# Layer 0 of a two-block transformer: gate tiles and modulation products set among the attention steps, and a reordered start

## The chip, the cores and the metric

The kernel runs on one core of a Trainium2 chip. It is written engine by engine: TensorE (PE) multiplies, VectorE (DVE) and ScalarE (ACT) work element by element, GpSimd (POOL) does elementwise work and issues some transfers, and SyncE (SP) issues the rest. Each engine runs its own list in order, and semaphores are what holds them together. The metric is the device time of one launch in microseconds. Lower is better.

## The reference

Two transformer blocks of two layers each work on 256 tokens of width 1024, all in float32. Only layer 0 of the first block is touched, with the prologue that leads to it:

```python
mod = silu_c @ w_mod[l] + b_mod[l]; mod_c = silu_cc @ w_mod[l] + b_mod[l]     # 1024 -> 6144, for the tokens and for the context
h  = modulate(rms_norm(x, norm1[l]), sh1, sc1);  hc = modulate(rms_norm(ctx, norm1[l]), csh1, csc1)
na_q, na_k, na_v, gq, gk, gv, ga, gb = split(h @ w_in[l])                     # and the same of hc
ya = window attention of 8 heads, 64 wide, with bias, over 256 tokens and 256 context tokens
ob = grouped attention of 8 query heads and 2 key heads, q and k normed per head and rotated
x  = x + g1 * ((sigmoid(ga) * (ya @ w_pa) + sigmoid(gb) * (ob @ w_pb)) @ w_o) # layer 0 does the same for the context
```

`ga` and `gb` are the gates, 1024 features each. The modulation is a product of one row per stream with a 1024 x 6144 matrix: it costs 24 MB of weights a layer and nearly no arithmetic.

## The kernel before, in words

**The plan.** `Plan` holds a list of items written out by hand. Every engine walks that list and does its own part of each item, in order. So the order of the `add` calls, and of the generators that make them, is the order on every engine. There is no scheduler behind it.

**Weights.** A weight piece is 128 x 2048 floats (1 MB) or less, loaded by SP into a ring of four slots (`piece`, L162). The load of piece n is issued when piece n - 3 has begun on TensorE (L1045 to L1053). A piece that is multiplied with h is split: ACT copies it, rounded, to `w_hi`, and DVE writes the rest over the slot as `ring_lo`; three products (hi by hi, lo by hi, hi by lo) replace one product in float32. `ahead` (ACT L1511, DVE L1983) does the splits up to the count that `look_ahead` (L175) wrote into the piece: one split piece ahead, if it lies at most three pieces further on. A modulation piece isn't split.

**Feature tiles.** `feat` (L488) makes tiles of 128 output features by 512 columns (256 tokens and 256 context tokens): 24 products of 128 x 512 in `product` (L1114), then a copy by ACT (L1644). Two tiles come from a 1 MB piece. The 16 gate tiles are eight pieces of `w_in`. Tiles are written into three PSUM banks in turn (`linear`, L158). The copies of gates 0 to 7, 8 to 11 and 12 to 15 go over the window attention's queries and keys, its values, and its bias.

**Modulation.** Unit j of `mod_unit` (L341) makes 2048 of the 6144 outputs from eight steps `mod` (L1228); a step is a 1 MB piece and four products of 32 columns wide weights side by side. DVE copies the sum, TensorE turns it onto the partitions (`mod_turn`, L1256), and DVE adds the bias. Unit 0 is made in the start. Unit 1 takes its pieces not from the ring but from `logits` and `prob_t`, which POOL fills by turns (`mod_loads`, L1898), each load when the buffer's last piece has been used.

**The start** (`first_tiles`, L587). ACT squares eight chunks, DVE adds six of them (L2010), TensorE sums over the partitions (L1166), and from the roots come the normed rows. `rows` are the modulated chunks of h (ACT L1568, DVE L2059 and L2051), two chunks at a time for the low part. `parts(i, c)` (L1213) adds chunk c to the two tiles of piece i. `mod_in` (L1182) and `turn` (L1194) make the modulation of each half of the chunks. The second half stands after tile piece 0's first four parts.

**Layer 0** (`first_block`, L655): two steps of unit 1, four key tiles with the other six among them, the tile of the grouped values, unit 1's turn, the window values (`tok`, L1300), and then attention. An attention step `att` is two heads by 128 queries; step i makes its scores (L1352), then the values of step i - 3 (L1378), then the turned probabilities of step i - 2 (L1363). DVE takes the scores from PSUM with the minimum (L2345, with bias L2347), ACT exponentiates (L1726), DVE inverts (L2357), POOL scales (L1918). Steps 0 to 7 and 16 to 23 have 512 keys, the others of the 32 have 256. Steps 0 to 4 run among the last five feature tiles (gk, gq), steps 5 to 18 beside the head norm (`head_sums` L1313, `head_spread` L1325), the rotation (`rope` L1333) and the eight steps of modulation unit 2, one at a time. From step 20 on each call is followed by one gate tile. `merge1` comes behind.

Of the kernel before, what the change touches and what calls it, by code (L numbers as in the profile page):

```python
# [13 lines left out]
P = 128  # L14
# [127 lines left out]
class Plan:  # L142

    def __init__(self):
        self.items, self.pieces, self.splits = [], [], []
        self.full, self.taken, self.lin, self.counts = [0] * 8, [0] * 8, 0, {}
        self.in_slot = [0] * RING
# [10 lines left out]
    def linear(self):  # L158
        self.lin += 1
        return self.fill((self.lin - 1) % LIN)  # L160
# [14 lines left out]
    def look_ahead(self):  # L175
        done = 0
        for p in self.pieces:
# [4 lines left out]
            if nxt and nxt.s < own + 1 and nxt.n <= p.n + RING - 1:  # L182
                done += 1
# [3 lines left out]
def hybrid_kernel(nc, xt, vec_d, con_d, tables_d, rpb, w, out):  # L187

    with ExitStack() as ctx:
# [151 lines left out]
        def mod_unit(l, j, aside=False, f=None, f2=None):  # L341
# [12 lines left out]
            add("mod_turn", l=l, j=j, of=f, f=f2 or fill(TURN_BANK))  # L354
# [232 lines left out]
        def first_tiles(f):  # L587
# [46 lines left out]
            parts(0, 0, 1, 2, 3)  # L634
            mod_in(1, (0, 0), (0, 1))
            parts(1, 0, 1)
            mod_in(1, (1, 0), (1, 1))
            parts(1, 2)
            turn(1)
            parts(1, 3)  # L640
# [14 lines left out]
        def first_block(l):  # L655
# [44 lines left out]
            for u in range(8):  # L700
# [8 lines left out]
            if l == 0:  # L709
                unit, loads = mod_unit(0, 1, True), mod_loads(0, (1,), (logits, prob_t), turned)  # L710
                some(loads, 2)
                first_tiles_out(first)
                in_turn(unit, loads, 2)
                for t in nk:
                    for i, _ in enumerate(t):
                        in_turn(unit, loads, 1 + i)
# [4 lines left out]
                some(unit, 1)  # L721
# [7 lines left out]
                unit = mod_unit(0, 2, f=linear(), f2=linear())  # L729
                head_squares(hn, 0, 1, 2, 3)  # L730
                att(g)
                some(unit, 1)
                head_squares(hn, 4)
                att(g)
                some(unit, 1)
                head_sums(hn)
                att(g)
                some(unit, 1)
                att(g)
                some(unit, 1)  # L740
                head_spread(hn, 0, 1, 2)
                att(g)
                some(unit, 1)
                head_spread(hn, 3, 4)
                att(g)
                some(unit, 1)
# [3 lines left out]
                some(unit, 1)  # L750
                rope(ropes[3:], 1, need=(hn["last"],))
                att(g)
                some(unit, 1)
                add("ahead", p=plan.pieces[-1])
                last_mod = unit
# [3 lines left out]
                some(last_mod, 1)  # L759
                while g["i"] < 19:  # L760
                    att(g)
            else:
# [299 lines left out]
        def _(pe):  # L1062
# [96 lines left out]
            def pe_first_norm(st):  # L1159
                n = st["n"]  # L1160
                room(n["f"])
                pe.wait_ge(first_added, KC - 2)
                pe.wait_ge(squares, KC)
                for t in range(4):
                    for c in (0, KC - 1):
                        mm = pe.matmul(ps[n["f"].bank][:, t:t + 1], y1[:, c * SQ + t * P:c * SQ + (t + 1) * P], ones[:, 0:1],  # L1166
                                       start=c == 0, stop=c == KC - 1)
# [5 lines left out]
            def pe_first_mod(st):  # L1173
# [5 lines left out]
                unread((22, 2, 0, 0, 0, 0, 0, 0)[i])  # L1179
# [1457 lines left out]
```

## Time and profile before

| | us |
|---|---|
| median of 3 runs (2540.3 to 2549.95) | 2547.2 |
| the profiled execution | 2547.93 |
| its span in the profile | 2546.1 |
| PE busy | 2465.5 (97%) |
| DVE busy | 1427.2 (56%) |
| ACT busy | 1132.8 (44%) |
| POOL busy | 360.0 (14%) |
| mean granted clock of TensorE | 0.988 |

The span is the profile's own; 1.8 us lie around it. A busy PE isn't a full one: matmuls overlap, their ends are modelled, and a matmul at the lower clock counts as busy for twice as long. So the stretches in which PE is less than full, or its granted clock less than 1, are what is to be looked for.

### The profile page before, as it was taken

What the parts mean: (1) busy time and instruction counts of PE and PEld (TensorE: products, weight loads), DVE (VectorE), ACT (ScalarE), POOL (GpSimd) and SP (SyncE); (2) the same over time, 40 slices, a digit from 0 to 9 for tenths busy, and PEclk for the clock granted to TensorE, in tenths of its full rate; (3) what the DMA queues carried; (4) which work ended last, traced back from release to release, by engine and by line L of the source; (5) the groups of instructions that cost most, each with busy time, mean ns of one, the idle gap of its engine ahead of it and who ended that gap; (6) DMA issues with size and microseconds to landing.
All of it is one profiled execution on the core that took longest, in us unless ns stands there. A gap on an engine that the chain in (4) does not pass through costs nothing.

```text
span 2546.1 us, 41134 instructions
## 1 busy us (share of the span) xinstructions
PE 2465.5 (97%) x17098; PEld 2207.8 (87%) x17098; DVE 1427.2 (56%) x2394; ACT 1132.8 (44%) x1960; POOL 360.0 (14%) x354
## 2 busy tenths in 40 slices
PE   8988999999999999999999998999999999999998
PEld 6753778888888877899999998999999998899998
DVE  5234335574446445555566567576556556657654
ACT  3243443421222535554454444465445444447443
POOL 0233313100001305200100000240000000024000
PEclk9997999999999999999999999999999999999999
DMA  7622123353444332345565453355455454335543
GB/s 289 225 87 87 61 83 133 115 172 134 150 170 167 133 100 83 133 166 177 171 210 185 165 166 119 128 180 182 167 191 189 167 190 139 115 125 196 183 163 136
DMA packets 82697, 390.32 MB, mean 153 GB/s; under 512 B 14992, under 2 KB 23472, under 8 KB 52176
## 3 DMA queue, kind: packets, MB, share of 16 engines
q1 hardware_dynamic: 73136, 347.78, 40.2%
q0 software_dynamic: 9376, 39.91, 4.5%
q8 instruction: 136, 2.23, 0.4%
q14 instruction: 49, 0.40, 0.1%
HBM read 386.62 MB, written 1.05 MB: 152 GB/s over the span
## 4 chain that ended last, share of the span: by engine, by line
PE 87%; DVE 6%; ACT 5%; issue 2%; DMA 1%; POOL 0%; SPq 0%; DVEq 0%; POOLq 0%; ACTq 0%
PE ps L1114 74%; PE ps L1300 2%; PE ps L1378 2%; DVE ring_lo L1991 2%; PE ps L1363 2%; PE ps L1352 2%; ACT logits L1726 1%; ACT w_hi L1521 1%; PE ps L1213 1%; ACT prob_t L1733 0%; DMA arena<-w_mod 0%; PE ps L1325 0%; PE ps L1228 0%; PE ps L1313 0%; PE ps L1147 0%
## 5 line engine op out<-in xcount | busy, mean ns | idle before, releaser
L1991 DVE TENSOR_TENSOR ring_lo<-ring,w_hi 128x1024 fp32r<-128x1024 f32 (+3 forms) x704 | 763.8, 1126 | 328.5 <-ACT w_hi L1521 328.4
L1114 PE MATMUL ps<-h_hi,w_hi 128*128 128x256 f32 (+1 forms) x3392 | 936.0, 307 | 3.4 <-issue 1.6
L1114 PE MATMUL ps<-h_lo,w_hi 128*128 128x256 f32 (+1 forms) x3392 | 923.3, 304 | 1.5 <-DVE h_lo L2166 1.5
L1521 ACT ACTIVATE w_hi<-ring 128x1024 fp32r<-128x1024 f32 (+3 forms) x704 | 633.2, 947 | 411.3 <-PE ps L1114 374.4
L1114 PEld LDWEIGHTS ps<-h_hi,w_hi 128*128 128x128 f32 x3392 | 648.0, 192 | 44.6 <-issue 18.3
L1114 PEld LDWEIGHTS ps<-h_lo,w_hi 128*128 128x128 f32 x3392 | 648.4, 192 | 26.0 <-DVE h_lo L2166 1.7
L1114 PE MATMUL ps<-h_hi,ring_lo 128*128 128x256 f32 (+1 forms) x3392 | 558.1, 303 | 2.5 <-DVE ring_lo L1991 2.5
L1114 PEld LDWEIGHTS ps<-h_hi,ring_lo 128*128 128x128 f32 x3392 | 480.7, 192 | 27.4 <-DVE ring_lo L1991 3.0
L1114 PE MATMUL ps<-hid_hi,w_hi 128*128 128x256 f32 (+1 forms) x1078 | 290.1, 299 | 0.0
L1114 PE MATMUL ps<-hid_lo,w_hi 128*128 128x256 f32 (+1 forms) x1078 | 289.5, 298 | 0.0
L1918 POOL TENSOR_SCALAR logits<-logits,stat 128x512 f32<-128x512 f32 (+2 forms) x140 | 161.3, 1165 | 593.7 <-DVE stat L2357 593.7
L1114 PEld LDWEIGHTS ps<-hid_hi,w_hi 128*128 128x128 f32 x1078 | 206.3, 191 | 7.6 <-issue 1.7
L1114 PEld LDWEIGHTS ps<-hid_lo,w_hi 128*128 128x128 f32 x1078 | 206.3, 191 | 6.0
L2250 DVE TENSOR_TENSOR prob_t<-prob_t,ps 128x256 f32<-128x256 f32 (+1 forms) x132 | 61.5, 466 | 266.3 <-issue 236.4
L1873 POOL TENSOR_TENSOR logits<-logits 128x256 f32<-128x256 f32 (+1 forms) x71 | 61.9, 872 | 1045.1 <-ACT logits L1542 822.0
L1114 PE MATMUL ps<-hid_hi,ring_lo 128*128 128x256 f32 (+1 forms) x1078 | 181.5, 298 | 0.0
L1726 ACT ACTIVATE logits<-logits,stat 128x512 f32<-128x512 f32 (+2 forms) x140 | 81.5, 583 | 186.1 <-DVE logits L2345 88.7
L1114 PEld LDWEIGHTS ps<-hid_hi,ring_lo 128*128 128x128 f32 x1078 | 153.1, 191 | 6.0
L1679 ACT ACTIVATE prob_t<-prob_t 128x256 f32<-128x256 f32 x88 | 36.7, 417 | 161.4 <-DVE prob_t L2243 161.4
L1352 PE MATMUL ps<-arena 64*128 64x512 f32 (+2 forms) x280 | 69.0, 529 | 9.2 <-DVE logits L2345 6.6
L1114 PE MATMUL ps<-y_lo,w_hi 128*128 128x256 f32 (+1 forms) x272 | 77.7, 308 | 0.0
L2280 DVE SCALAR_TENSOR_TENSOR x_res<-ps,mod,x_res 128x256 f32<-128x256 f32 x64 | 29.1, 480 | 84.2 <-PE ps L1114 84.2
(287 smaller groups left out, 2416.0 us busy)
## 6 DMA issues: line engine op xcount, KB each, us to landing
ring<-w_ffn_in SPq DMA_DIRECT2D x132, 1024.0 KB, 4.9
ring<-w_ffn_out SPq DMA_DIRECT2D x96, 704.0 KB, 4.0
ring<-w_in SPq DMA_DIRECT2D x36, 1024.0 KB, 4.8
ring<-w_w_in SPq DMA_DIRECT2D x28, 1024.0 KB, 4.9
bias_t<-w_mod POOLq DMA_DIRECT2D x24, 1024.0 KB, 5.4
ring<-w_up SPq DMA_DIRECT2D x16, 576.0 KB, 3.7
ring<-w_mod SPq DMA_DIRECT2D x8, 1024.0 KB, 5.6
ring<-w_pab SPq DMA_DIRECT2D x8, 1024.0 KB, 4.9
```

What stands on the lines that cost most here:

```text
L1114: mm = pe.matmul(ps[fs[k].bank][:, at_col:at_col + n], (hi_w if wpart == "hi" else lo_w)[0:rows, at[k]:at[k] + P], hi if part == "hi" else ...
L1300: mm = pe.matmul(ps[f.bank][:, 0:st["n"]], at_T(part, c, T, t * P, P), wt[:, at:at + st["n"]], start=c == 0 and part is h_hi and wt is w_h ...
L1352: pe.matmul(ps[f.bank][:, 0:sp_["nk"]], p["q"][a, t * P:(t + 1) * P], p["k"][a, k0:k0 + sp_["nk"]], start=True, stop=True).then_inc(psum_f ...
L1363: mm = pe.transpose(ps[f.bank][:, c * P:(c + 1) * P], logits[:, o:o + P], ident)
L1378: mm = pe.matmul(ps[f.bank][DH * h:DH * h + DH, o:e], p["v"](c, h), prob_t[:, h * 1024 + c * S + o:h * 1024 + c * S + e], start=start, sto ...
L1521: act.activation(w_hi[q.s % 2][:, h * n:(h + 1) * n], ring[q.slot][:, h * n:(h + 1) * n], ACT.Copy)\
L1679: act.activation(t, t, ACT.Silu).then_inc(silu_done, 1)
L1726: act.activation(lg, lg, ACT.Exp, scale=-1.0, bias=stat[:, o:o + 1], accum_out=stat[:, 4 + o:5 + o])\
L1873: pool.tensor_tensor(sq_sum[:, o:n], sq_sum[:, o:n], sq[j % 2][:, o:n], ALU.add).then_inc(sq_added, 1)
L1918: pool.tensor_scalar(lg, lg, stat[:, 8 + (a % 2) * 2 + h:9 + (a % 2) * 2 + h], None, ALU.mult)\
L1991: dve.tensor_tensor(ring_lo[q.slot][:, c], ring[q.slot][:, c], plain(w_hi[q.s % 2][:, c]), ALU.subtract)\
L2250: dve.tensor_tensor(tmp[2 + i % 2][:, 0:T], t, ps[u.bank][:, 0:T], ALU.mult).then_inc(psum_taken[u.bank], 1)
```

## The change

Eight edits, by place:

- Layer 0 has no unit 1 among the key tiles any more and no POOL loads for it. Both units 1 and 2 come from the ring, in pairs of steps, between attention steps 5 and 17, each turned a step later.
- Between those steps stand five gate tiles. The first four are pieces of 512 KB for one tile each, gates 12 to 15. The other twelve tiles follow in the order 0, 1, 2, 3, 8 to 11, 4 to 7. The last eleven are spread over the last 18 calls of `att`, so that seven of these have none.
- While a unit adds up, its PSUM bank is held: `linear` uses the other two. `mod_turn` takes a bank of `linear` too.
- `look_ahead` allows a split two pieces further on, not three, and `split_next` asks for the split of the piece behind a pair of steps.
- In the start the second half's modulation stands one chunk earlier and its turn two chunks earlier.
- DVE adds all eight squares; TensorE sums one chunk, not two, in four products in place of eight.
- DVE makes each chunk's low part at once, not two chunks' together.
- The first filling products are 20, not 22.

```diff
     def linear(self):
         self.lin += 1
+        if (self.lin - 1) % LIN == self.held:
+            self.lin += 1
         return self.fill((self.lin - 1) % LIN)
...
-            if nxt and nxt.s < own + 1 and nxt.n <= p.n + RING - 1:
+            if nxt and nxt.s < own + 1 and nxt.n <= p.n + 2:
...
-            add("mod_turn", l=l, j=j, of=f, f=f2 or fill(TURN_BANK))
+            add("mod_turn", l=l, j=j, of=f, f=f2 or linear())
...
-            parts(0, 0, 1, 2, 3)
+            parts(0, 0, 1, 2)
             mod_in(1, (0, 0), (0, 1))
-            parts(1, 0, 1)
+            parts(0, 3)
             mod_in(1, (1, 0), (1, 1))
-            parts(1, 2)
+            parts(1, 0)
             turn(1)
-            parts(1, 3)
+            parts(1, 1, 2, 3)
...
-            for u in range(8):
+            if l == 0:
+                for c in range(12, 16):
+                    half = f[7 + c // 2].rearrange("p (k n) -> p k n", k=KC)[:, :, c % 2 * P:c % 2 * P + P]
+                    gate_tiles.append(feat("gate", half, [c], T, length=KC * P, l=l))
+            for u in range(8) if last else (0, 1, 4, 5, 2, 3):
                 gate_tiles.append(feat("gate", f[7 + u], [2 * u, 2 * u + 1], T, l=l))
...
-                unit, loads = mod_unit(0, 1, True), mod_loads(0, (1,), (logits, prob_t), turned)
-                some(loads, 2)
                 first_tiles_out(first)
-                in_turn(unit, loads, 2)
-                for t in nk:
-                    for i, _ in enumerate(t):
-                        in_turn(unit, loads, 1 + i)
+                run_all(*nk)
...
-                some(unit, 1)
                 tok("nav", w["w_nav"][l], 2, SLOT, 512, SQ, nav)
...
+                unit = held_unit(1)
                 head_squares(hn, 0, 1, 2, 3)
                 att(g)
-                some(unit, 1)
+                mods(unit)
                 head_squares(hn, 4)
                 att(g)
-                some(unit, 1)
+                mods(unit)
                 head_sums(hn)
                 att(g)
-                some(unit, 1)
+                mods(unit)
                 att(g)
-                some(unit, 1)
+                mods(unit)
+                split_next()
                 head_spread(hn, 0, 1, 2)
                 att(g)
-                some(unit, 1)
+                turn(unit)
+                next(gates)
+                unit = held_unit(2)
                 head_spread(hn, 3, 4)
                 att(g)
-                some(unit, 1)
+                mods(unit)
+                split_next()
+                att(g)
+                next(gates)
                 rope(ropes[:3], 1, need=(hn["last"],))
...
                 att(g)
+                turn(unit)
+                next(gates)
+                left, tiles = len(g["steps"]) + 4 - g["i"], 11
+                for i in range(left):
                     att(g)
+                    some(gates, (i + 1) * tiles // left - i * tiles // left)
...
-                pe.wait_ge(first_added, KC - 2)
-                pe.wait_ge(squares, KC)
+                pe.wait_ge(first_added, KC - 1)
                 for t in range(4):
-                    for c in (0, KC - 1):
-                        mm = pe.matmul(ps[n["f"].bank][:, t:t + 1], y1[:, c * SQ + t * P:c * SQ + (t + 1) * P], ones[:, 0:1],
-                                       start=c == 0, stop=c == KC - 1)
+                    mm = pe.matmul(ps[n["f"].bank][:, t:t + 1], y1[:, t * P:(t + 1) * P], ones[:, 0:1], start=True, stop=True)
...
-                for c in range(1, KC - 1):
+                for c in range(1, KC):
...
-                if c % 2:
-                    low(c - 1)
-                    low(c)
+                low(c)
```

## Rows read from the trace of the kernel before

**Rows 1.** Page, part 4: the chain that ended last, by engine.

```profile
PE 87%; DVE 6%; ACT 5%; issue 2%; DMA 1%; POOL 0%; SPq 0%; DVEq 0%; POOLq 0%; ACTq 0%
```

**Rows 2.** Windows: stretch, length, busy of PE, PEld, DVE, ACT, POOL; clock, DMA, GB/s.

```profile
0.00:58.98 58.98, 50.87 (x279) 36.62 (x279) 30.80 (x61) 22.43 (x37) 2.20 (x7) 0.94 0.77 306
...
58.98:100.10 41.12, 38.66 (x194) 25.17 (x194) 6.71 (x7) 9.12 (x13) 5.57 (x8) 0.96 0.75 259
100.10:161.00 60.90, 60.42 (x280) 45.45 (x280) 18.41 (x34) 21.17 (x38) 22.89 (x16) 1.00 0.31 103
161.00:193.10 32.10, 24.91 (x128) 10.35 (x128) 13.59 (x30) 16.09 (x36) 12.38 (x8) 0.99 0.43 127
193.10:251.60 58.50, 46.27 (x204) 22.05 (x203) 27.46 (x86) 21.97 (x63) 20.71 (x20) 0.77 0.23 75
251.60:371.20 119.60, 119.60 (x611) 88.95 (x610) 42.29 (x101) 50.05 (x109) 33.22 (x28) 1.00 0.21 71
```

**Rows 3.** Timeline of PE, 58 to 79 us: unit 1 and a key tile.

```profile
58.98 1.06 PE L1228 MATMUL ps<-logits,silu_c 128*32 128x512 f32 x8
...
60.83 0.50 PE L1114 MATMUL ps<-h_hi,w_hi 128*128 128x512 f32 x1
...
76.72 1.94 PE L1228 MATMUL ps<-logits,silu_c 128*32 128x512 f32 x8 [2.46 <-DMA logits<-w_mod]
```

**Rows 4.** Timeline of PE, 266 to 310 us: attention steps between gate tiles.

```profile
274.27 1.13 PE L1352 MATMUL ps<-arena 64*128 64x512 f32 x4
275.33 1.95 PE L1378 MATMUL ps<-prob_t,arena 128*64 128x256 f32 x16
277.21 1.09 PE L1363 MATMUL ps<-con,logits 128*128 128x128 f32 x8
278.05 0.48 PE L1114 MATMUL ps<-h_hi,w_hi 128*128 128x512 f32 x1
...
307.40 0.70 PE L1352 MATMUL ps<-arena 64*128 64x256 f32 x4
```

**Rows 5.** Timeline of PE, 170 to 194 us: work between steps, and its waits.

```profile
173.23 3.61 PE L1313 MATMUL ps<-arena,con 128*16 128x512 f32 x8 [1.79 <-ACT prob_t L1733]
...
182.55 1.22 PE L1352 MATMUL ps<-arena 64*128 64x256 f32 x4 [1.78 <-DVE stat L2347]
...
189.80 3.38 PE L1325 MATMUL ps<-arena,con 16*128 16x512 f32 x6 [1.19 <-ACT prob_t L1733]
```

**Rows 6.** Timeline of PE, 240 to 246 us: a step with no tile before it.

```profile
242.67 2.09 PE L1352 MATMUL ps<-arena 64*128 64x512 f32 x4 [1.29 <-DVE logits L2345]
```

**Rows 7.** Windows of 2 us, PE alone: length, busy time, clock, DMA share, GB/s.

```profile
192.00:194.00 2.00, 2.00 (x6) 0.63 0.74 286
...
206.00:208.00 2.00, 2.00 (x16) 0.95 0.00 0
```

**Rows 8.** Groups of DVE by form, 160 to 370 us: taking 512-key scores.

```profile
L2345 DVE TENSOR_SCALAR_CACHE_REDUCE logits<-ps 128x512 f32<-128x512 f32 x16 | 10.4, 686 | 23.1 <-PE ps L1363 23.1
```

**Rows 9.** Issues of transfers, 0 to 420 us: KB each, median us to landing.

```profile
ring<-w_mod SPq DMA_DIRECT2D x8, 1024.0 KB, 5.6
...
prob_t<-w_mod SPq DMA_DIRECT2D x1, 1024.0 KB, 28.0
```

**Rows 10.** Timeline, 7 to 50 us: the start.

```profile
7.36 1.93 SPq L1037 DMA_DIRECT2D prob_t<-w_mod  x1
...
9.99 4.67 DVE L2010 TENSOR_TENSOR arena<-arena 128x512 f32<-128x512 f32 x6 [0.54 <-ACT arena L1548]
...
15.22 1.95 PE L1166 MATMUL ps<-ones,arena 128*128 128x1 f32 x16
...
28.34 0.95 PE L1213 MATMUL ps<-h_lo,w_hi 128*128 128x512 f32 x2 [1.12 <-DVE h_lo L2051]
...
46.51 0.70 PE L1213 MATMUL ps<-h_hi,w_hi 128*128 128x512 f32 x2 [0.26 <-ACT h_hi L1568]
...
48.78 0.73 PE L1213 MATMUL ps<-h_lo,w_hi 128*128 128x512 f32 x2 [1.11 <-DVE h_lo L2051]
```

More of the change, by code:

```diff
@@ L146, in __init__ @@
         self.full, self.taken, self.lin, self.counts = [0] * 8, [0] * 8, 0, {}
-        self.in_slot = [0] * RING
+        self.in_slot, self.held = [0] * RING, None
     def add(self, kind, **kw):
@@ L728, in first_block, with mods, turn, held_unit @@
                 hn = head_norm(norm_chunks(), "sum_heads", hroot)
-                unit = mod_unit(0, 2, f=linear(), f2=linear())
+                def mods(unit):
+                    some(unit, 2)
+                def turn(unit):
+                    plan.held = None
+                    some(unit, 1)
+                def held_unit(j):
+                    f = linear()
+                    plan.held = f.bank
+                    return mod_unit(0, j, f=f)
+                def split_next():
+                    add("ahead", p=plan.pieces[-1])
+                unit = held_unit(1)
                 head_squares(hn, 0, 1, 2, 3)
                 att(g)
-                some(unit, 1)
+                mods(unit)
                 head_squares(hn, 4)
                 att(g)
-                some(unit, 1)
+                mods(unit)
                 head_sums(hn)
                 att(g)
-                some(unit, 1)
+                mods(unit)
                 att(g)
-                some(unit, 1)
+                mods(unit)
+                split_next()
                 head_spread(hn, 0, 1, 2)
                 att(g)
-                some(unit, 1)
+                turn(unit)
+                next(gates)
+                unit = held_unit(2)
                 head_spread(hn, 3, 4)
                 att(g)
-                some(unit, 1)
+                mods(unit)
+                split_next()
+                att(g)
+                next(gates)
                 rope(ropes[:3], 1, need=(hn["last"],))
@@ L749, in first_block @@
                 att(g)
-                some(unit, 1)
+                mods(unit)
+                split_next()
                 rope(ropes[3:], 1, need=(hn["last"],))
                 att(g)
-                some(unit, 1)
-                add("ahead", p=plan.pieces[-1])
-                last_mod = unit
+                next(gates)
+                att(g)
+                mods(unit)
+                split_next()
+                att(g)
+                next(gates)
                 g2 = attention([gq_pair(i, 0, 0, SQ) for i in range(4)] + [gq_pair(i, S, S, S) for i in range(4)])
@@ L758, in first_block @@
                 att(g)
-                some(last_mod, 1)
-                while g["i"] < 19:
+                mods(unit)
+                split_next()
+                att(g)
+                turn(unit)
+                next(gates)
+                left, tiles = len(g["steps"]) + 4 - g["i"], 11
+                for i in range(left):
                     att(g)
+                    some(gates, (i + 1) * tiles // left - i * tiles // left)
             else:
```

2 lines of the change are left out of this document (1 added, 1 removed).

## Prediction

> **What bounds the kernel now.** I read the page's chain of waits first: 87% of the chain that ended last is TensorE [rows 1]. A change of order can then only win where TensorE is less than full, so the second view is its busy time and granted clock by stretch [rows 2]. From 371 us on the change touches nothing. In the four stretches that it does touch, TensorE's 0.00 to 58.98 us is the start, 58.98 to 100.10 is modulation unit 1 with the key tiles, 161.00 to 193.10 and 193.10 to 251.60 are the attention steps without feature tiles, and 251.60 to 371.20 is the same attention with a gate tile in each step. The reader is to see that the last one is full (119.6 of 119.6 us at clock 1.00), while in the two before it 7.2 and 12.2 us are idle and the second has clock 0.77. The timeline then gives the price of each piece of work and the releaser of each wait.
>
> **Prices at full clock.** A feature tile between steps takes 5.65 us: 278.05 to 283.70, the end being the sum of the pieces in the row before it and its neighbours, and about 5.5 us net of the overlap with what precedes it. An attention step costs 1.06 us of scores with 512 keys and 0.63 with 256, 1.88 of values in every second step (half of it with 256 keys), and 0.84 to 1.0 of turned probabilities (half with 256) [rows 4]. Two modulation steps take 58.98 to 60.83, so 0.93 each [rows 3]. The head sums take 173.23 to 177.6, 4.4 us for five products of 512 columns, and the five spread products another 4.3; five rotations of half that width take 2.1 [rows 5]. A modulation turn is about 0.9.
>
> **Part 1, the start.** Three edits on the path of the first tiles.
> (a) The squares. DVE makes seven additions where it made six: they took 4.67 us, so 0.78 more, ending at 15.4. TensorE's sum started at 15.22, behind a modulation step, and took 1.95 us for 16 recorded products; it now starts 0.2 us later and has half of them, 1.0 us less [rows 10]. Gain 0.7 us.
> (b) Low parts one by one. TensorE waits 1.12 us at 28.34 for the first h_lo, which DVE makes behind the second chunk's two scalings; those lie now behind it. Half a pair of scalings is 0.7, so gain 0.7 [rows 10].
> (c) The second half's modulation and turn stand earlier. The waits of 0.26 and 1.11 us at 46.51 and 48.78 came because the turn had only one part of a tile behind it. Now it has three, 4.2 us, which cover DVE's amplitudes and the first rows. Gain 1.4, plus some 0.3 of low clock behind (b). The cost is a landing: the last of the four pieces is issued at 7.36 and lands 28.0 us later, at 35.4 [rows 9, 10]. TensorE reaches its products at about 35.6 by my count (it stood at 39.5 before). So it costs nothing, or up to 1.5 us if the landing slips by so much.
> Sum: 3.1 us, between 1 and 3.5. The two filling products less are 0.3 us ahead of a transfer that ends the wait in either case: 0.
>
> **Part 2, unit 1 leaves the key tiles.** The stretch of 41.12 us holds five tiles (four of keys, one of values for the grouped heads), eight modulation steps, a turn, and a wait of 2.46 us for a transfer into `logits`, after which the clock is low: the next step takes 1.94 us in place of 1.06 [rows 2, 3]. Five tiles alone are 5 x 5.65 = 28.2 us. Gain 12.9 us. What hides the pieces' transfers and splits: each slot is loaded three pieces ahead, 11 us or more, against 5.6 us of landing [rows 9], and the values' split has a tile of 5.5 us over it. POOL's load of the tables and the window bias, which stood behind eight loads of unit 1, starts some 25 us earlier, so attention step 0 doesn't wait for it. From 84 to 145 us (before: 100 to 161) the work is the same and TensorE full.
>
> **Part 3, the attention stretch.** From 161.00 to 251.60, 90.6 us, the work at full clock is: steps 5 to 19 with scores 7 x 1.06 + 8 x 0.63 = 12.5, turned probabilities 11.2, values 9.4; eight modulation steps 7.4; turn 0.9; head sums 4.4; spreads 4.3; rotations 2.1. Sum 52.2 us. So 38.4 us are waits and low clock. The following 119.6 us have none. The change puts unit 1's eight steps and its turn here, 8.3 us more work, and lets the gate tiles fall on the waits. What stays:
> - Steps 5 to 9 have no tile yet. Their longest waits were 1.79, 1.78 and 1.19 us [rows 5], beside shorter ones; a second modulation step of 0.93 falls on each. I take 4 us to stay.
> - Steps 9 to 17 with five tiles, ten of the 16 modulation steps behind or before a tile. The rotations still wait for DVE's three operations a chunk, and the turned probabilities for the banks these hold. 3.5 us.
> - The last 18 calls have 11 tiles, so seven calls have none. There the next scores wait until DVE has taken the last ones: two instructions of 0.686 us [rows 8]; such a wait was 1.29 us [rows 6]. With 512 keys I take 1.6 us, with 256 keys 1.1: about 8.5 us. Bounds: nothing (the tiles on both sides cover it, as in the last stretch of [rows 2]) and 3 us a call (POOL's scaling becomes late too), 21 us.
> - Low clock. Behind waits of 1.78 and 1.19 us within 10 us the clock fell from 1.00 to 0.63 in the window at 192, and rose to 0.95 in that at 206 [rows 5, 7]. With a tile in every step it never fell [rows 2]. I take one or two falls of 3 to 4 us, each costing half of that: 2 us.
> Sum 18 us. Part 3 gives 38.4 - 18 - 8.3 = 12.1 us. The ends are 22 (waits of 8 us in all) and 0 (30 us).
>
> The Trainium skill, "TensorE: Matmul & The Clock Gate", section "A second HAM failure mode: psum-queue depth-cycling", speaks against mixing such steps: frequent short idle times between groups of matmuls make the clock swing, and what is paid is the way back up. By that rule seven bare calls and the pairs of modulation steps would each cost a fall. Here the trace agrees for the bare steps (0.77) and not for the mixed ones (1.00) [rows 2].
>
> **Other edits.** Splits two pieces ahead in place of three: `look_ahead` matters only where two unsplit pieces lie between. Behind the rule ACT would stand at a transfer only just issued, with the exponentials of the next step queued behind it, and DVE, POOL and TensorE behind those. With the split asked for behind the pair, the piece was issued four or five us of work earlier, and lands in 5.6 us at most for 1 MB [rows 9]. Cost 0, at most 1 us per tile, 5 us. The held bank: a tile's bank comes free when ACT has copied it, long before the second next tile; 0. POOL loses eight transfers; SP's queue takes them behind the same waits for slots; counted in part 3.
>
> **The sum.** 3.1 + 12.9 + 12.1 = 28.1 us. The profiled execution took 2547.93 us, 0.7 above the median of the runs; 2547.9 - 28.1 = 2519.8. I say 2520.
>
> **Rivals.**
> - *The clock stays low* in the stretch with the five new tiles (by the page's rule above it could). In 193 to 251 us 46% of the time was at the lower of its two levels, 1.2 GHz [rows 2]. The work of steps 9 to 17 with five tiles is 58 us; at the same share it takes 75, so 15 more than I counted: 2535. For it: waits remain. Against it: density, and [rows 2] on the last stretch. 8%.
> - *ACT and DVE stand at splits and tile copies* that are now in among the exponentials. A tile is copied only when TensorE has finished it, and the next exponentials are behind; if each of 12 tiles costs 1.7 us, that is 20 us: 2540. For it: ACT was busy half of 161 to 193 [rows 2]. Against it: with a tile a step TensorE had no such wait. 8%.
> - *The ring can't feed it*: slower than before. Unit 1's eight pieces come on top, so 21 pieces (16 of modulation, five of tiles) go through a ring with three in flight while the stretch should last 94 us. With 5.6 us to landing that is 21 x 5.6 / 3 = 39 us, hidden. It becomes the bound above 13 us to landing, and the change a loss above 17; when ten pieces were queued together one landed after 28.0 us [rows 9], which would give 21 x 28 / 3 = 196 us, 102 more: 2622. Against it: DMA share 0.23 to 0.43 there. 3%.
> - *Parts 1 and 2 alone*: the mixed steps win nothing, since DVE's chain sets their pace. 2547.9 - 16 = 2532, in the range; 10%.
>
> **How the numbers follow.** The forecast has 71%, with its own range of 2511 to 2529 from the bounds. The last rival's 2532 still belongs; the clock rival's 2535 and the third's 2540 are left out in part. Range 2509 to 2535. About 0.5%, 13 us, is what a measurement of this kernel can tell from no change, so faster means below 2534.5: forecast 71 + last rival 9 + half of the clock rival 4 + one part of the ACT rival 1 = 85%. Within 0.5%: 12%. Slower: 3%.
>
> **What would show it right or wrong.** The first key tile should begin near 56 us and the window values near 84, the first attention step near 112. Between there and the end of the gates at about 343 us the clock should be above 0.9 in every 20 us, with TensorE's waits for `logits` (DVE) at 8 to 10 us and none for a `w_mod` piece. DVE and ACT should have no busy time more than before. Wrong it would be if modulation steps wait for transfers, if the products of the last start piece wait over 1.5 us, if ACT's wait for a ring piece holds exponentials, or if the stretch behind the gates differs from 2174.8 us by over 3 us.

## The result, and the profile after

The changed kernel took 2528.95 us (median of 4 runs, 2528.08 to 2532.0) against 2545.01 for the kernel before beside it (2540.3 to 2549.95): ratio 0.9934, 95% interval 0.9918 to 0.9949, so 13 to 21 us less. The forecast was 2520 with a range of 2509 to 2535. Direction and range hold; of the 28 us of the sum, 16 came by the medians. That the range held owes much to part 1 and part 2: part 3, 12.1 us in the sum, gave next to nothing. The profiled execution took 2528.57 us, 19.4 less than the one before.

Windows of the kernel after, cut at its own landmarks (length; busy time of PE, PEld, DVE, ACT, POOL; granted clock, DMA share, GB/s):

```profile
0.00:54.60 54.60, 46.56 (x266) 33.93 (x267) 31.80 (x62) 22.32 (x37) 0.50 (x5) 0.97 0.73 292
54.60:81.80 27.20, 27.20 (x121) 22.45 (x120) 7.11 (x6) 8.30 (x12) 7.30 (x6) 1.00 0.56 196
81.80:142.80 61.00, 60.51 (x282) 45.59 (x281) 17.58 (x33) 21.72 (x39) 20.36 (x13) 1.00 0.28 86
142.80:174.80 32.00, 28.22 (x158) 11.78 (x158) 13.94 (x32) 17.07 (x38) 12.40 (x8) 0.95 0.61 192
174.80:252.20 77.40, 73.09 (x381) 46.49 (x381) 37.03 (x105) 31.89 (x81) 24.07 (x23) 0.96 0.53 180
252.20:351.20 99.00, 91.34 (x474) 66.00 (x474) 33.98 (x90) 40.01 (x94) 29.98 (x26) 1.00 0.16 54
351.20:2526.80 2175.60, 2127.30 (x15411) 1981.37 (x15409) 1287.13 (x2074) 991.91 (x1665) 263.56 (x267) 0.99 0.46 156
```

They answer to [rows 2]. The start ends at 54.60 (58.98 before), the five tiles take 27.2 us in place of 41.1 (in the profile of the new start alone, where unit 1 still stands among them, they take 41.7 at clock 1.00; in the change with the old start 27.2), the stretch with steps 0 to 4 is as it was, and `merge1` begins at 351.20 in place of 371.20. Behind it the two kernels take 2175.6 and 2174.9 us. The reader is to see the sixth line: the clock is 1.00, and yet PE is idle for 7.7 of 99 us, in a stretch that was full before.

PE's waits of the kernel after, 142 to 351 us (total, times, longest):

```profile
PE ps L1392 <- ACT prob_t L1762: 3.4, 5, 0.7
PE ps L1381 <- DVE logits L2372: 2.5, 6, 0.5
PE ps L1407 <- ACT prob_t L1762: 2.4, 3, 0.9
PE ps L1407 <- DVE prob_t L2397: 2.0, 1, 2.0
```

In this kernel L1381 is the scores, L1392 the turned probabilities, L1407 the values and L1146 the tiles; ACT's L1755 is the exponentials, L1762 its copy of the turned probabilities out of PSUM, L1770 its copy of the values' result; DVE's L2372 takes the scores, and L2397 is DVE's copy of the turned probabilities. In this list the waits for ACT's copy are larger than those for DVE's scores, which was the only wait that I had put down for a bare call. But the list leaves out what stands inside a group of recorded matmuls, and there more of the wait for DVE is hidden, as the next rows show.

The part of the chain of waits that runs through one bare call, an `att` without a tile (start, us, engine, what):

```profile
257.16 0.60 PE ps L1392 x4
257.88 0.37 DVE logits L2372
258.61 1.52 ACT logits L1755 x4
260.13 0.27 ACT arena L1770
260.40 0.49 ACT prob_t L1762
261.02 1.06 PE ps L1392 x8
262.09 5.49 PE ps L1146 x24
```

And the timeline of PE at the same place:

```profile
257.09 1.09 PE L1392 MATMUL ps<-con,logits 128*128 128x128 f32 x8
258.63 1.74 PE L1381 MATMUL ps<-arena 64*128 64x512 f32 x4 [0.44 <-DVE logits L2372]
261.02 1.06 PE L1392 MATMUL ps<-con,logits 128*128 128x128 f32 x8 [0.66 <-ACT prob_t L1762]
```

The bare call before it (245.28 us) reads alike, and there the rows of TensorE's weight loads show what the group of four scores hides:

```profile
245.28 0.29 PEld L1381 LDWEIGHTS ps<-arena 64*128 64x128 f32 x2 [0.69 <-DVE logits L2372]
245.88 0.29 PEld L1381 LDWEIGHTS ps<-arena 64*128 64x128 f32 x2 [0.32 <-DVE logits L2372]
```

What DVE waited for, in the call above (its timeline):

```profile
257.88 0.69 DVE L2372 TENSOR_SCALAR_CACHE_REDUCE logits<-ps 128x512 f32<-128x512 f32 x1 [6.68 <-PE ps L1392]
```

Read it so: two waits follow each other. The first is for DVE. TensorE's next scores need the banks that DVE empties one after the other, so the group takes 1.74 us where it takes 1.13 between tiles [rows 4]: with the 0.44 us ahead of it, 1.05 us. DVE itself had been idle for 6.68 us, until L1392: its code waits for the turn, because step i's scores go into the half of `logits` from which TensorE turns step i - 2's probabilities.

The second wait is for ACT. TensorE turns a step's probabilities into a bank. The bank comes free when ACT has copied it, but ACT's list has two exponentials of the next step (1.52 us) and L1770 ahead of that copy: 0.66 us more.

From one turn to the next are 3.93 us, with 1.02 us of turning (the turn at 151.05 us is followed by a modulation step at 152.07) and 1.06 of scores in them: a bare call with 512 keys costs 1.85. The seven cost 1.85, 1.85, 2.07, 1.4, 1.6, 1.6 and 2.03, in sum 12.4. In the first six DVE's scores make 5.3 us of it and ACT's copy 4.2; the last is a wait for DVE's copy, told below. With a tile of 5.5 us in between all of this is covered.

### The profile page after: what moved, and what is told of

Read it like the earlier page. It is cut to its first block, busy times and chain, and to the rows that moved or that the text cites. A ratio compares the mean times of both kernels' runs of the same rounds, so it can differ in the third digit from the quotient of the medians.

```text
span 2526.8 us, 41125 instructions
## 1 busy us (share of the span) xinstructions
PE 2454.2 (97%) x17086; PEld 2207.6 (87%) x17086; DVE 1428.6 (57%) x2399; ACT 1133.2 (45%) x1964; POOL 358.2 (14%) x346
## 3 DMA queue, kind: packets, MB, share of 16 engines
HBM read 386.62 MB, written 1.05 MB: 153 GB/s over the span
## 4 chain that ended last, share of the span: by engine, by line
PE 86%; DVE 6%; ACT 5%; issue 2%; DMA 0%; POOL 0%; DVEq 0%; POOLq 0%; SPq 0%; ACTq 0%
PE ps L1146 75%; PE ps L1329 2%; DVE ring_lo L2020 2%; PE ps L1407 2%; PE ps L1392 2%; ACT logits L1755 1%; PE ps L1381 1%; ACT w_hi L1550 1%; PE ps L1242 1%; ACT prob_t L1762 0%; PE ps L1179 0%; PE ps L1342 0%; DVE arena L2500 0%; PE ps L1276 0%; DVE logits L2372 0%
## 5 line engine op out<-in xcount | busy, mean ns | idle before, releaser
L2020 DVE TENSOR_TENSOR ring_lo<-ring,w_hi 128x1024 fp32r<-128x1024 f32 (+4 forms) x708 | 765.1, 1122 | 334.7 <-ACT w_hi L1550 334.4
L1146 PE MATMUL ps<-h_hi,w_hi 128*128 128x256 f32 (+1 forms) x3392 | 935.4, 308 | 4.2 <-issue 1.6
L1146 PE MATMUL ps<-h_lo,w_hi 128*128 128x256 f32 (+1 forms) x3392 | 922.9, 304 | 1.5 <-DVE h_lo L2193 1.5
L1550 ACT ACTIVATE w_hi<-ring 128x1024 fp32r<-128x1024 f32 (+4 forms) x708 | 633.6, 943 | 401.8 <-PE ps L1146 365.2
L1146 PEld LDWEIGHTS ps<-h_hi,w_hi 128*128 128x128 f32 x3392 | 648.0, 192 | 41.2 <-issue 14.5
L1146 PEld LDWEIGHTS ps<-h_lo,w_hi 128*128 128x128 f32 x3392 | 648.3, 192 | 26.4 <-DVE h_lo L2193 1.7
L1146 PE MATMUL ps<-h_hi,ring_lo 128*128 128x256 f32 (+1 forms) x3392 | 558.9, 303 | 2.5 <-DVE ring_lo L2020 2.5
L1146 PEld LDWEIGHTS ps<-h_hi,ring_lo 128*128 128x128 f32 x3392 | 481.5, 192 | 27.4 <-DVE ring_lo L2020 3.0
L1146 PE MATMUL ps<-hid_hi,w_hi 128*128 128x256 f32 (+1 forms) x1078 | 290.1, 299 | 0.0
L1146 PE MATMUL ps<-hid_lo,w_hi 128*128 128x256 f32 (+1 forms) x1078 | 289.5, 298 | 0.0
L1146 PEld LDWEIGHTS ps<-hid_hi,w_hi 128*128 128x128 f32 x1078 | 206.3, 191 | 7.6 <-issue 1.7
L1146 PEld LDWEIGHTS ps<-hid_lo,w_hi 128*128 128x128 f32 x1078 | 206.3, 191 | 6.0
L1146 PE MATMUL ps<-hid_hi,ring_lo 128*128 128x256 f32 (+1 forms) x1078 | 181.5, 298 | 0.0
L1755 ACT ACTIVATE logits<-logits,stat 128x512 f32<-128x512 f32 (+2 forms) x140 | 81.5, 583 | 178.0 <-DVE logits L2372 80.5
L1146 PEld LDWEIGHTS ps<-hid_hi,ring_lo 128*128 128x128 f32 x1078 | 153.1, 191 | 6.0
L1146 PE MATMUL ps<-y_lo,w_hi 128*128 128x256 f32 (+1 forms) x272 | 77.7, 308 | 0.0
L1392 PEld LDWEIGHTS ps<-con,logits 128*128 128x128 f32 x386 | 42.2, 143 | 35.7 <-issue 31.8
```

Of the source, the lines that this page charges most:

```text
L1146: mm = pe.matmul(ps[fs[k].bank][:, at_col:at_col + n], (hi_w if wpart == "hi" else lo_w)[0:rows, at[k]:at[k] + P], hi if part == "hi" else ...
L1392: mm = pe.transpose(ps[f.bank][:, c * P:(c + 1) * P], logits[:, o:o + P], ident)
L1550: act.activation(w_hi[q.s % 2][:, h * n:(h + 1) * n], ring[q.slot][:, h * n:(h + 1) * n], ACT.Copy)\
L1755: act.activation(lg, lg, ACT.Exp, scale=-1.0, bias=stat[:, o:o + 1], accum_out=stat[:, 4 + o:5 + o])\
L2020: dve.tensor_tensor(ring_lo[q.slot][:, c], ring[q.slot][:, c], plain(w_hi[q.s % 2][:, c]), ALU.subtract)\
```

## The experiments

"Layer 0" below is the time at which `merge1` begins: 371.2 us before, 351.2 after. Medians are given beside those of the kernel before, measured with it. Times within a run are those of one profiled execution.

**The start alone.** The kernel before with the five edits of the start (order of the second half, eight squares added by DVE, one chunk summed, low parts one by one, 20 filling products).

```diff
-            parts(0, 0, 1, 2, 3)
+            parts(0, 0, 1, 2)
             mod_in(1, (0, 0), (0, 1))
...
-                if c % 2:
-                    low(c - 1)
-                    low(c)
+                low(c)
```

> The kernel before with the start's edits alone (the sums, the low parts one by one, the second half's modulation and turn earlier, 20 filling products). By the traces of both kernels the first key tile began 4.4 us earlier (54.6 for 59.0), so: 4.4 us faster than before, the key tiles beginning at 54.6 to 55.5. The rival is that part of this came from POOL's loads of unit 1, which are still here and share the transfers: then 3 us or less, with a wait in the start for a transfer.

Measured: 2542.45 against 2546.76 us, ratio 0.9988 (0.9977 to 0.9999). The first step of unit 1 stands at 55.26 us in place of 58.98. Some 3 to 4 us, as the sum had it; the interval alone would allow 0.3 to 6.

**The change without its start.** The kernel after with the same five edits undone.

```diff
-            parts(0, 0, 1, 2)
+            parts(0, 0, 1, 2, 3)
             mod_in(1, (0, 0), (0, 1))
...
-                low(c)
+                if c % 2:
+                    low(c - 1)
+                    low(c)
```

> The changed kernel with the start of before. If the start is worth the same on this side, 4.4 us slower than the changed kernel, that is 12 us faster than before; the key tiles begin at 59. If the parts help each other the difference isn't that of the start-only kernel.

Measured: 2534.51 us, ratio 0.9945 (0.9931 to 0.9959); layer 0 ends at 356.7, 5.5 later than with the new start. By the ratios (0.9945 for 0.9934) the difference is 3 us, and the intervals overlap. Taken together the start is worth 3 to 5.5 us, and no run shows that anything behind it gives them back.

**ACT copies first.** The kernel after with ACT's work of a call in another order: the copy of the turned probabilities ahead of the exponentials. This tells theory Q (ACT's queue holds the bank) from D (DVE's taking of the scores sets the stall).

```diff
-                if at < len(steps):
-                    exps(at)
                 if at >= 3 and steps[at - 3]["t"] == 1:
-                    copy_y(at - 3)
+                    full(steps[at - 3]["p"]["V"])
                 if 2 <= at < len(steps) + 2:
                     copy_turned(at - 2)
+                if at < len(steps):
+                    exps(at)
+                if at >= 3 and steps[at - 3]["t"] == 1:
+                    copy_y(at - 3)
```

> The changed kernel, but in each attention step ScalarE copies step i - 2's turned probabilities out of PSUM before it exponentiates step i, not behind it; this holds for all attention, in every layer of both blocks. Theory Q (queue on ScalarE): in a call without a tile TensorE stands for 1.4 to 2.1 us because the PSUM bank of the next turned probabilities is freed by that copy, behind two exponentials of 0.72 and the read of their sums, 1.5 us together. Then the seven stalls (12.4 us) fall to about 0.5 each, 8 us or more, and other layers' attention gains a few more: 10 to 20 us faster than the changed kernel. Theory D (VectorE, as forecast): the next scores wait for VectorE to take the last ones, so ScalarE's order matters little: within 2 us of the changed kernel.

Measured: 2518.66 us, ratio 0.9885 (0.9872 to 0.9899), an interval that lies below that of the change. Layer 0 ends at 342.0, 9.2 earlier. A bare call of this kernel, PE's timeline:

```profile
237.27 1.09 PE L1392 MATMUL ps<-con,logits 128*128 128x128 f32 x8
238.81 1.73 PE L1381 MATMUL ps<-arena 64*128 64x512 f32 x4 [0.45 <-DVE logits L2374]
240.47 1.09 PE L1392 MATMUL ps<-con,logits 128*128 128x128 f32 x8
```

The wait for ACT is gone and the turns are 3.20 us apart, 0.73 less; what is left, 1.12 us, is the wait for DVE's scores (L2374 here), as large as it was: 0.45 us ahead of the group and 0.6 inside it. POOL's scaling of the probabilities that are turned next ends at 240.39 us, 0.1 before the turn, by a span that the profile gives only roughly: a faster DVE would win little here before POOL's work sets the pace. Over the whole program PE's two waits for that copy, 7.0 and 3.8 us after the change, are now

```profile
PE ps L1407 <- ACT prob_t L1762: 1.0, 2, 0.5
...
PE ps L1392 <- ACT prob_t L1762: 0.4, 1, 0.4
```

Q holds: ACT's order is worth far more than the 2 us that D allowed. But the stalls did not fall to about 0.5 us as Q had it. In a bare call ACT's queue holds 0.73 us of 1.85 and DVE's taking of the scores the larger part, 1.12, so D names a real cause that ACT's order doesn't touch. Outside layer 0, the stretch with layer 1's attention, which runs the same code, is 3.5 us shorter: 373.1 us from 884.14 us on, 376.6 from 894.15 after the change.

**ACT copies first, in the kernel before.** The same edit without the change.

> The kernel before with the same new order on ScalarE. Theory Q: its steps 5 to 18 have no tile, so about twelve such stalls shrink by 1 us or more, and the granted clock falls less in that stretch: 12 us or more faster than before, and the changed kernel's gain over it is smaller than 16 us. Theory D: within 2 us of before.

Measured: 2531.33 us, ratio 0.9939 (0.9926 to 0.9952), layer 0 ends at 353.6. One reordering on ACT gives as much as the whole change. In layer 0 of the profiled executions it is worth 17.6 us without the change and 9.2 with it. The two can't be set against each other as they stand: by the windows' clock the kernel before lost 13.8 us to low clock between step 5 and the gates and this one 6.8, while with the change the loss hardly differs (4.7 and 3.5). By the ratios the reordering is worth 15.5 us without the change and 12.5 with it. That the mixed tiles had covered a part of the same wait fits this, but how much isn't shown.

**No early tiles.** The kernel after without the five gate tiles among the rotations; all 16 are spread over the last 18 calls, so that two are bare.

```diff
                 turn(unit)
-                next(gates)
                 unit = held_unit(2)
...
-                left, tiles = len(g["steps"]) + 4 - g["i"], 11
+                left, tiles = len(g["steps"]) + 4 - g["i"], 16
```

> The changed kernel without its five early gate tiles: all 16 tiles fall on the last 18 calls, so two of these are bare in place of seven, and between steps 9 and 17 there are only modulation steps, rotations and spreads. Theory F (a fixed number of fillers): TensorE's stalls come per call that has nothing between it and the next, 1.4 to 2.1 us each; the tiles only move them, so the kernel is within 4 us of the changed one, and what the change gains it gains by filling calls with the second unit's steps and by freeing the key tiles. Theory G (the forecast's): the early tiles take the place of 38 us of waits and low clock, and without them the early stretch stands as in the kernel before: 8 us or more slower than the changed kernel, with the clock near 0.8 there.

Measured: 2531.04 against 2547.73 us, ratio 0.9931 (0.9914 to 0.9947), against 0.9934 for the whole change; layer 0 ends at 353.8. From 142.8 to 252.2 us the clock was

```profile
142.80:252.20 109.40, 97.18 (x502) 0.89 0.49 155
```

and 0.95 in the same window of the kernel after. So in these two executions the clock is higher where the early tiles stand, and the bare calls that they leave behind, seven in place of two, take the gain back: the stall is moved and not removed.

**Look-ahead of three.** The kernel after with the old rule for splits.

```diff
-            if nxt and nxt.s < own + 1 and nxt.n <= p.n + 2:
+            if nxt and nxt.s < own + 1 and nxt.n <= p.n + RING - 1:
```

> The changed kernel with splits allowed three pieces further on, as before. Then the split of the next half gate piece stands in the list of the tile before it, at a piece whose load is issued only when the first modulation step of that pair begins, and ScalarE waits at it with the next exponentials behind. The stretch from step 9 to step 17 should be 5 us longer or more, with ScalarE waiting for ring transfers; if the forecast is right that this costs nothing where the loads come early, within 1 us.

Measured, one run: 2545.75 us; layer 0 ends at 367.0, 15.8 later than after. ACT's timeline:

```profile
206.50 1.15 ACT L1550 ACTIVATE w_hi<-ring 128x512 fp32r<-128x512 f32 x2 [6.76 <-DMA ring<-w_w_in]
```

ACT stands 6.76 us at the split of a piece that has only just been issued, and over the program this wait is 22.6 us in four times. Exponentials and copies stand behind it, and PE's longest wait for DVE's scores is 3.1 us in place of 0.5. In that execution the old rule ate nearly the whole gain of layer 0. Only some 6 us of it are more idle time of TensorE there; some 10 are low clock, which this one run can't tie to the waits. The whole is still 14 us above the slowest run of the kernel after.

**A tile one call earlier.** The last but one of the calls that have work on TensorE, bare, gets the tile of the call behind it. In the kernel after the last bare call waits 2.03 us for DVE's copy, L2397, behind DVE's split of the result, which in turn waits for ACT behind a gate tile's copy; the chain of the kernel after:

```profile
336.67 0.60 ACT arena L1673
337.27 0.53 ACT yb_hi L1784
337.82 0.69 DVE y_lo L2410
338.51 0.34 DVE prob_t L2397
339.10 1.08 PE ps L1407 x8
```

```diff
-                    some(gates, (i + 1) * tiles // left - i * tiles // left)
+                    some(gates, (i + 1) * tiles // left - i * tiles // left + {15: 1, 16: -1}.get(i, 0))
```

> The changed kernel with that tile moved one call earlier and nothing else. The wait of 2.03 us and the 2.03 us between the turned probabilities and it are one stall: merge1 begins 2 us earlier. If the last step's values need their own time whatever stands before them, 0.

Measured, one run: 2525.14 us; layer 0 ends at 349.1, 2.1 earlier, and the wait of 2.03 is gone.

> The changed kernel with ScalarE's copy ahead of the exponentials, and with the tile behind the last but one call moved one call earlier, since the last call has no work on TensorE and two tiles stand side by side there while call 33 is bare and costs 2.03 us of wait for VectorE's copy. Expected 2 us faster than the kernel with the copy order alone, 14 us faster than the changed kernel. If the wait has another cause it stays at the next call.

With both edits: 2515.16 us, ratio 0.9873 (0.9857 to 0.9889), layer 0 ends at 340.7. This is the best version found, some 32 us below the kernel before; from ACT's order alone (0.9885) the times don't tell it apart, the trace of layer 0 does by 1.3 us.

**The start taken apart.** The kernel before with the sum alone (eight squares added, one chunk summed), and with the low parts alone.

> The kernel before with VectorE adding all eight squares and TensorE summing one chunk in four products; nothing else. The products that spread the root began 0.84 us earlier in the changed kernel (16.98 for 17.82), and this is the only edit ahead of them but for two filling products: so they begin at 17.0 here, and the first products of the first tile 0.8 to 1.0 us earlier than before.

> The kernel before with VectorE making each chunk's low part at once; nothing else. By the forecast the first low part is 0.7 us earlier, and the wait of 1.12 us at 28.34 falls to 0.4, the one of 1.11 us at 48.78 likewise, so the key tiles begin 1.4 us earlier. The rival: VectorE's next chunk is later by as much, and the wait moves to the third chunk, as in the changed kernel, where 0.85 us stood at 30.42; then 0.5 us or less in the first half.

The first: 2549.14 against 2550.53 us, one run each. The first tile's products came later than before, not earlier, because the clock was low from 13.0 to 23.2 us in that execution; it says nothing on the sum. The second: 2539.96 us, one run; the first step of unit 1 stands at 56.81 us, 2.2 earlier than before, of which 1.7 is the low clock that the kernel before had at 28.7 to 32.1 us. The rest of the difference isn't this edit's by anything that the trace shows. PE's timeline:

```profile
27.33 0.73 PE L1213 MATMUL ps<-h_lo,w_hi 128*128 128x512 f32 x2 [0.32 <-DVE h_lo L2051]
31.21 0.74 PE L1213 MATMUL ps<-h_lo,w_hi 128*128 128x512 f32 x2 [0.84 <-DVE h_lo L2051]
...
46.54 0.73 PE L1213 MATMUL ps<-h_lo,w_hi 128*128 128x512 f32 x2 [0.32 <-DVE h_lo L2051]
```

The 1.12 us at the first low part become 0.32, and 0.84 come up at a later chunk: in the first half the wait only moves. In the second half 1.11 become 0.32 and nothing comes up.

**ACT's order without early tiles.** The kernel of "no early tiles" with ACT's order.

> The kernel without the five early tiles, with ScalarE's copy ahead of the exponentials. With the old order it was level with the changed kernel, so by theory F (fillers only move the stalls) it should be level with the kernel that has the new order and the early tiles, 12 us faster than the changed kernel, within 3. If the early tiles are worth something once the stalls are short, by keeping the granted clock up between steps 9 and 17 (it fell there for 24 us without them and for 10 with them), it is 4 us or more slower than that one.

Measured: 2515.92 against 2544.78 us, ratio 0.9886 (0.987 to 0.9902); with early tiles it was 0.9885. With either order on ACT the early tiles are worth nothing that these runs can tell.

**Both copies first.** The best version with DVE's copy, too, ahead of its taking of the scores.

```diff
+                if 2 <= at < len(steps) + 2:
+                    copy_turned(at - 2)
                 if at < len(steps):
                     softmax_in(at)
-                if 2 <= at < len(steps) + 2:
-                    copy_turned(at - 2)
```

> The kernel with ScalarE's new order and the shifted tile, and VectorE too copies its head's turned probabilities before it takes the new scores. If what is left of a bare call's stall is the second bank, freed by VectorE behind two scores of 0.69 us, this gives 2 us or more again. If it is the scores themselves (theory D, now in second place), the copy ahead of them costs 0.42 to 0.69 us in each call without a tile, in all layers: 2 us or more slower.

Measured: 2534.26 us, ratio 0.9959 (0.9945 to 0.9974): 19 to 22 us worse than the best version, half of it in layer 0 (350.5) and half in layer 1's attention. The timeline of DVE at a bare call, and then of PE:

```profile
246.07 0.69 DVE L2399 COPY prob_t<-ps 128x512 f32<-128x512 f32 x1 [0.96 <-PE ps L1392]
246.68 0.68 DVE L2374 TENSOR_SCALAR_CACHE_REDUCE logits<-ps 128x512 f32<-128x512 f32 x1
```

```profile
244.87 1.09 PE L1392 MATMUL ps<-con,logits 128*128 128x128 f32 x8
247.42 1.73 PE L1381 MATMUL ps<-arena 64*128 64x512 f32 x4 [1.46 <-DVE logits L2374]
249.08 1.09 PE L1392 MATMUL ps<-con,logits 128*128 128x128 f32 x8
```

The same move that helps on ACT hurts on DVE. DVE's copy is of the second head and needs the whole turn; its taking of the first head's scores needs only the first head's half of it, which is done 0.4 us earlier. So the scores are taken 0.4 us later for the turn and 0.6 for the copy now ahead of them. TensorE waits 1.46 us for its scores' bank where it waited 0.45, and the exponentials start later by the same: the turns are 4.21 us apart in place of 3.20. The expectation had this second branch and its sign, and put it at 2 us or more.

## Why the prediction was right, and where it was off

Direction and range came out, but by luck in part: the two sure parts carried it, and the third, whose account of the bare calls was incomplete, gave a seventh of its sum. By its own steps, in layer 0, between the two profiled executions: part 1 gave 4.4 us (3.1 forecast), part 2 13.9 (12.9), part 3 1.7 (12.1). Together 20.0, and 0.7 lost behind.

**Part 1.** (a) The spread of the roots begins at 16.98 us (17.82 before): 0.8, forecast 0.7. (b) Forecast 0.7 for the low parts: the wait of 1.12 became 0.32, but in the first half 0.85 came up two parts later, as with the low parts alone. I had followed the first wait and not asked what DVE does next. (c) The waits of 0.26 and 1.11 us in the second half are gone and the last start piece's products, at 35.40, wait for nothing: right. What is over the forecast is mostly low clock: about 1.7 us at 28.7 to 32.1 us in the execution of the kernel before, of which the forecast had counted 0.3.

**Part 2.** Five tiles in 27.2 us, 5.44 each, all busy and at full clock, where I had 5.65. No wait for the split or a transfer: the mechanism as told, and the tiles' price a little too large. The length is the same in the change with the old start (27.2), and 41.7 us at clock 1.00 with the new start alone, so it isn't an accident of the clock; but no run moved unit 1 and did nothing else.

**Part 3** is where the forecast failed. From step 5 to `merge1` it had 210.2 us less 12.1, so 198.1: 180.1 of work and 18 of waits and low clock. The stage took 208.5. The 10.4 us more:
- The bare calls: forecast 8.5 us for seven, measured 12.4. The term was in the sum, and its bounds (0 and 21) held it, but one of its causes was missing. I took it from the wait of 1.29 us before scores [rows 6] and DVE's two instructions [rows 8]. That wait is there, 1.05 us a call with 512 keys where I had 1.6, in sum 5.3 us. What the sum had nowhere is ACT's copy behind two exponentials, 4.2 us in six calls, and DVE's copy in the last, 2.0; 0.9 is left over. The runs with ACT's order show it: 0.73 us less a call, and 9.2 us less in layer 0 in all.
- Low clock: forecast 2 us. It was low from 166.9 to 170.3 and from 177.1 to 183.9 us, 10.2 us, which at half speed cost 5.1. The windows of 2 us (length, PE busy, clock, DMA share, GB/s) at the second place:

```profile
176.00:178.00 2.00, 1.81 (x8) 0.78 1.00 336
178.00:180.00 2.00, 2.00 (x12) 0.50 0.85 324
180.00:182.00 2.00, 2.00 (x9) 0.50 0.00 0
182.00:184.00 2.00, 2.00 (x6) 0.51 0.24 70
184.00:186.00 2.00, 2.00 (x10) 1.00 0.65 192
```

  Before each place stand waits of under 1 us (0.92 and 0.88; 0.33, 0.56 and 0.19) with steps too short to cover ACT. The forecast said one or two falls; there were two places, the second twice as long.
- The other waits were about 9.0 us for 7.5, and the rest, 2 us, I put down to work counted too low.

Two of the signs that the forecast had named came out against it: from 166 to 186 us the clock was 0.74, where it was to stay above 0.9 in every 20 us, and TensorE's listed waits for `logits` are 2.5 us, where 8 to 10 were expected.

The price of a call with a tile was right: none waits. What I got wrong is what [rows 2] could prove. That a stretch with a tile in each step is full shows that a tile covers the stall, not how large the stall is; its size stood in the bare steps of 161 to 193, where 1.79 and 1.19 us were already put down to ACT's copy [rows 5]. I read these two rows as waits of the head norm and didn't ask what ACT had ahead of that copy. The plain bare call stood in the trace of before as well, a few rows behind the one that I took, with both of its waits:

```profile
246.60 1.34 PE L1363 MATMUL ps<-con,logits 128*128 128x128 f32 x8
248.39 1.73 PE L1352 MATMUL ps<-arena 64*128 64x512 f32 x4 [0.45 <-DVE logits L2345]
250.78 1.06 PE L1363 MATMUL ps<-con,logits 128*128 128x128 f32 x8 [0.66 <-ACT prob_t L1733]
```

**The clock among bare calls.** From 252.20 to 351.20 us six of the seven bare calls, with idle times of 0.27 to 2.03 us and 7.7 in all, lie among ten tiles, and the clock stays at 1.00; among the paired modulation steps and the rotations it was 0.95 and 0.96. By the Trainium skill ("TensorE: Matmul & The Clock Gate", section "A second HAM failure mode: psum-queue depth-cycling") frequent short idle times make it swing: the trace agrees for the second kind of steps and not for the first. The prediction set the same rule against the last stretch of the kernel before; that stretch had no idle time at all (119.6 of 119.6 us), so it said nothing on the rule.

**Look-ahead and ring.** Cost 0 was right for the new rule. But I had weighed the edit only as a possible cost, where it is a condition of the rest: with the old rule 15.8 of the 20.0 us in layer 0 were gone in the one execution seen. No product of `w_mod` waited for its piece after 142 us, and one weight load did, for 0.6 us, so the ring fed it.

**The rivals.** "Parts 1 and 2 alone" named 2532 and had 10%; with 1.7 us from part 3 it is nearer to what happened than the forecast's 12.1, and its reason, DVE's chain behind the attention steps that sets their pace, was half right: in a bare call it is DVE's taking of the scores and ACT's copy together. ACT at splits and tile copies (2540) showed in one place, the 2.03 us at 339.10, and not in twelve. The clock rival (2535) had the right sign: 3 us more than counted, not 15, and of the two places only the second lies where the five tiles stand. The ring didn't hold.

**Behind the gates** 0.7 us more, within the 3 us that I allowed. Over the first 450 us, where the clock was 1.00 in both executions, the two kernels agree to 0.1 us; the larger piece, 2.9 us, is the passage from layer 0 to layer 1's first tiles (774.4 to 928.4 us), at clock 0.96 after and 0.99 before, and other pieces give 2.2 of it back. The code there didn't change.

## What to carry to other kernels

When TensorE waits for a PSUM bank, look up in the releaser's own list what stands ahead of the instruction that frees it, and for which earlier event that one waits; on an engine in order the copy that frees a bank goes ahead of long work on other data, unless that work frees a bank which is wanted sooner, as DVE's taking of the scores did. A recorded group of matmuls can hide a wait inside it: compare its length with that of the same group where nothing waits. Filler laid among stalling steps wins only what it covers and leaves bare steps elsewhere if there is not enough of it: count the bare ones and price them before believing a gain. Before a new order of loads, check the rule that decides when in-order engines touch them.

## What the runs showed that I had not expected

The places where the clock falls differ between executions of one program. The kernel before took 2538.57 to 2552.81 us over the comparisons here. Its steps from 193.10 to 251.60 (58.5 us, clock 0.77, [rows 2]) took 52.0 us at clock 0.83 with the same code in the kernel with the new start alone, which window of PE reads (length, busy, clock, DMA share, GB/s)

```profile
189.50:241.50 52.00, 40.77 (x193) 0.83 0.24 81
```

That is why this kernel's profile ends layer 0 at 361.1, 10.1 us earlier than before's, though its start gave 3.7 of them. A single execution, and any difference between two profiles over a stretch with low clock, is uncertain by some 5 us here. Part 3's 1.7 us is such a difference. With the start at 3 to 5.5 us and part 2 at 14, the interval of 13 to 21 for the whole leaves part 3 between 6.5 lost and 4 gained: which of these is open, that it isn't 12 is not.
